# A per-row scalar for GpSimd's head weights, and relus of a score unit that are planned apart

## The reference

```
r = jax.nn.relu(jnp.einsum('bqhe,ble->bqhl', qi, ki_all))
score = jnp.einsum('bqhl,bqh->bql', r, wi)          # wi: one weight per query and head
score = jnp.where(adm, score, -jnp.inf)             # chunk-causal
_, idx = lax.top_k(score, topk)                     # topk = 256
...                                                 # attention over the chosen keys
```

## Time and profile before

| | |
|---|---|
| median of 3 runs | 5120.09 us (5118.19 to 5121.09) |
| profiled execution: span from first to last instruction | 5121.8 us |
| busy in the span: PE, DVE, ACT, POOL | 85%, 68%, 67%, 32% |
| stage one ends, next stage begins | about 2489 us into the span |

### The profile page before, as it was taken

How to read it: one execution, slowest core, us unless ns; L and a number is a source line. 1 busy time by engine, 2 the same in 40 slices (tenths; PEclk the granted TensorE clock), 3 DMA queues, 4 the chain that set the end, 5 groups by cost and what they waited for, 6 DMA issues and landing times. The chain is left out here.

```text
span 5121.8 us, 78325 instructions
## 1 busy us (share of the span) xinstructions
PE 4351.6 (85%) x26505; PEld 2716.9 (53%) x26505; DVE 3484.2 (68%) x6644; ACT 3455.7 (67%) x6887; POOL 1618.2 (32%) x1358
## 2 busy tenths in 40 slices
PE   6767778777677877777689999989999999989999
PEld 3334434443333433434366777767777777754444
DVE  1266778888797988989477777787776778625111
ACT  1578788888697787974378888868788885520100
POOL 1345556666647866677310000000000000000000
PEclk9888889888788888988799999999999999999999
DMA  6211111100011011101421111110110010044422
GB/s 143 61 51 45 38 38 36 35 33 36 22 44 39 33 37 44 42 32 46 152 70 56 51 42 39 40 53 31 34 40 28 28 40 24 12 119 134 118 94 103
DMA packets 201975, 276.98 MB, mean 54 GB/s; under 512 B 50496, under 2 KB 134176, under 8 KB 201056
## 3 DMA queue, kind: packets, MB, share of 16 engines
q1 hardware_dynamic: 198624, 271.81, 16.8%
q10 hardware_dynamic: 2960, 0.17, 0.0%
HBM read 156.73 MB, written 114.16 MB: 53 GB/s over the span
## 5 line engine op out<-in xcount | busy, mean ns | idle before, releaser
L595 PE MATMUL bank<-w,x 128*128 128x512 f32 (+1 forms) x2848 | 1256.8, 597 | 23.6 <-DVE w L940 13.5
L1042 DVE TENSOR_SCALAR_CACHE_REDUCE ties<-score,cand 128x512 int8<-128x512 f32 (+13 forms) x448 | 1110.6, 2479 | 123.2 <-POOL score L916 107.9
L595 PEld LDWEIGHTS bank<-w,x 128*128 128x128 f32 x2848 | 575.9, 206 | 612.7 <-issue 547.4
L806 ACT ACTIVATE act_junk<-score,a_cand,a_sign 128x384 int8<-128x384 f32 (+13 forms) x420 | 879.4, 2094 | 14.0
L1833 DVE CUSTOM_DVE_ANT_0 row<-bank,mask 128x512 f32<-128x512 f32 (+3 forms) x1024 | 622.6, 639 | 179.8 <-PE bank L1572 178.5
L613 PE MATMUL bank<-kiT,qi 128*128 128x512 f32 (+3 forms) x1136 | 395.3, 490 | 408.6 <-ACT relu L736 206.4
L1539 POOL TENSOR_TENSOR near_bias<-table,mask 128x2048 f32<-128x2048 f32 (+1 forms) x32 | 129.5, 4048 | 1763.9 <-DVE part L1833 1748.3
L1767 ACT ACTIVATE pT<-bank 128x512 f32<-128x512 f32 (+2 forms) x704 | 368.7, 524 | 426.2 <-PE bank L1588 424.0
L1669 ACT ACTIVATE row<-row,top 128x1024 f32<-128x1024 f32 (+7 forms) x640 | 632.8, 990 | 4.0 <-DVE top L1846 4.0
L1588 PE MATMUL bank<-ident,row 128*128 128x128 f32 x4224 | 593.7, 281 | 26.4 <-DVE pT L1944 19.5
L1572 PE MATMUL bank<-kT,qb 64*128 64x256 f32 (+1 forms) x4352 | 608.4, 396 | 8.7 <-DVE part L1833 5.4
(11 more groups left out here) (255 smaller groups left out, 4882.6 us busy)
## 6 DMA issues: line engine op xcount, KB each, us to landing
qk_t<-ring SPq DMA_DIRECT2D x66, 256.0 KB, 2.0
gates<-ring SPq DMA_DIRECT2D x66, 256.0 KB, 2.0
gate<-gates SPq DMA_DIRECT2D x33, 512.0 KB, 3.4
out<-x_in SPq DMA_DIRECT2D x33, 512.0 KB, 2.9
x<-in_x_prompt SPq DMA_DIRECT2D x32, 512.0 KB, 3.7
mixed<-mixT SPq DMA_DIRECT2D x64, 256.0 KB, 2.1
mix_in<-mixed SPq DMA_DIRECT2D x32, 512.0 KB, 4.2
x_in<-in_x_prompt SPq DMA_DIRECT2D x32, 512.0 KB, 3.8
```

Source lines behind the costliest of these rows:

```text
L595: ins = pe.matmul(p_bank[n % 2][:, 0:n1 - n0], held[:, c * P:(c + 1) * P], w[:, c, n0:n1], start=(c == 0), stop=(c == KC - 1))
L806: tick(act.activation(junk, row, ACT.Sign, bias=c, scale=back, accum_out=a_sum[:, :]))
L1042: n = tick(dve.tensor_scalar(ties[:, 0:width], row, c.bitcast(F32), 0.0, ALU.is_ge, ALU.add, accum_out=counts[:, i:i + 1]))
```

## The change

The weight is one value per row (a column of 128 values). Before, it is broadcast along the row and used as a second tensor in a `tensor_tensor`; after, it is the scalar operand of a `tensor_scalar`. The additions at L912 stay as they are. In ACT's generator the four relus of a unit get due times that are 1.8 us of planned time apart.

```diff
+RELU_GAP = 1.8
...
-                            for _ in relu_unit(t - 1, slot):
-                                yield us_at(t, slot + 0.6)
+                            for h, _ in enumerate(relu_unit(t - 1, slot)):
+                                yield us_at(t, slot + 0.6) + RELU_GAP * h
...
-                        r, weighs = relu[at % 3][:, 0:n], weight[:, u % 2, h:h + 1].to_broadcast([P, n])
+                        r, weighs = relu[at % 3][:, 0:n], weight[:, u % 2, h:h + 1]
                         pool.wait_ge(s_rl, at + 1)
                         if h == 0:
                             pool.wait_ge(s_wi, u + 1)
-                            pool.tensor_tensor(to, r, weighs, ALU.mult).then_inc(s_pa, 1)
+                            pool.tensor_scalar(to, r, weighs, None, ALU.mult).then_inc(s_pa, 1)
                         else:
-                            k = tick(pool.tensor_tensor(r, r, weighs, ALU.mult))
+                            k = tick(pool.tensor_scalar(r, r, weighs, None, ALU.mult))
                             pool.wait_ge(s_pool, k)
                             pool.wait_ge(s_pa, at)
                             pool.tensor_tensor(to, to, r, ALU.add).then_inc(s_pa, 1)
```

## The result

The changed kernel takes 5223.03 us (median of 4 runs, 5221.86 to 5224.29) against 5120.59 before (median of 4 runs, one more than in the table above): ratio 1.0197, 95% interval 1.0182 to 1.0211. That is 102 us more. The forecast was 5041 us, faster; neither the range nor the sign holds.

The account below looks back on a forecast made before the run. ACT, waiting at relus for POOL, was taken to bound stage one. Gains of 51 us (1305 to 2340), 20 (700 to 1305) and 8 (last step) make 79: 5120 - 79 = 5041 us, range 4965 to 5110.

Parts of the forecast that it names:

- the scalar form is no shorter: Rival on POOL's multiply: a column as scalar may take as long, only the planning acts; 5099 us, chance 0.05.
- the one-column row: Profile row on POOL: a tensor_scalar of one column, 0.19 us elsewhere, took 1.18 us beside a DVE compare.
- the 20-column row: Profile row on POOL: a tensor_scalar of 20 columns, 0.27 us, used in estimating the scalar multiply at 512 columns.
- The path: Stage one, 1305 to 2340: ACT is the path, going over to POOL where ACT stands at a relu, 153 us.
- nearly gone: Sign on ACT: waits behind the first multiply (L907) would nearly vanish; 30 of 35.4 us from 1305 to 2340.
- (c): ACT, 1305 to 2340: ten long waits, 75.8 us, with POOL held beside DVE's scan; planned tests take off 14 us.
- Shifted more than thinned: Planning in ACT's order: a place between tests still has about four relus; counted at nothing.
- (a): ACT, 1305 to 2340: a unit's fourth relu waiting for POOL's first multiply (L907); 30 of 35.4 us go.
- (b): ACT, 1305 to 2340: ordinary waits behind the addition (L912), POOL still at the last unit; 33 of 41.6 us go.
- Slower: evacuations behind the fourth relu: Rival, 150 to 1305: late relus delay evacuations, reaching PE's projection banks and ACT; 5162 us, chance 0.08.
- The waits pass on: Rival, stage one: PE's and DVE's fixed orders take over, only 35 us gained; 5085 us, chance 0.18.

Follow-up runs that it names:

- experiment 1: The two parts separately: the scalar multiply alone, an edit of the changed kernel, 5291.2 us; the planning alone, an edit of the kernel before, 5090.8 us.
- experiment 2: Kernel before with sixteen extra operations on POOL at the start of stage one, 128 and 512 columns, each waited for: 5127.6 us (one run).
- experiment 3: Kernel before with eight other tensor_scalar forms on POOL at the start, 128 and 512 columns, each waited for: column with multiply-add 0.69 us, multiply-max 1.93 us.

## Why the prediction was wrong

**The step that failed** is the price of the scalar multiply. It said 0.72 us, "no more than the addition with two full tensors, 1.27 us" as the upper end. It measured 1.56 us for 512 columns and 0.60 for 128, which is 2.5 ns per column. I had put the 0.88 ns per column of a memset onto a `tensor_scalar` of 20 columns: an operation that only writes lends no slope to one that reads and computes. The upper end rested on the thought that one long input can't cost more than two. Nothing in the trace showed that, and it is false here. With 1.56 the unit is 2.1 us longer, not 1.3 shorter. Even the prediction's own upper end lost 0.9 us per unit, yet no case was made of it: "the scalar form is no shorter" stopped at the same length, so no case held the result. Its sign of being wrong, a multiply of over 1 us, is the one that came. The same place also hid the cure: the one-column row is a two-operation form, the 20-column row a one-operation form, and I used both as if they were one.

The Trainium skill's figure cited there (GPSIMD Engine Reference, Performance versus the Vector engine), 768 ns for 512 elements in a tight loop, is met by neither form: 1.56 us with one operation, 0.69 with two, which is below it. The measurements decide.

**The path was read rightly.** With the multiply at 0.69 us, near the 0.72 of the prediction, and with the planning, the time is 5047 us and the gain 79 us: the forecast 5041 and its 79. Stage one ends at 2406.88, near 2410. Two more of its signs came in that run, from 1305 to 2340: ACT's waits behind the additions are 79.8 us (about 70 forecast), and DVE is busy 915 of 1035 us, 88% (above 87% forecast). The waits behind the first multiply are 20.5 us there, more than "nearly gone". That the sum fits so well is partly luck: the unit by itself gave 56 to 66 us, where the steps say 70 without (c), and the planning gave 13.

**The planning was mis-sized.** I counted it at nothing beside 14 us of (c). It gives 34 us with the old multiply, 64 with the slow one and 13 with the fast one. "Shifted more than thinned" was wrong for what matters: a fourth relu behind a test mostly no longer waits for the first multiply. These waits fell from 133 to 42 in experiment 1. And the gain did not come through (c): with the planning alone, ACT's waits of over 3.5 us behind POOL from 1305 to 2340 sum to 75.4 us, against 75.8 before. With the fast form the sum is 70.5 without the planning and 58.7 with it. (Of the ten waits in that sum one, 6.1 us, stands behind L907 and not L912; the prediction has all ten behind L912. It changes neither (a) nor (b) by more than some 6 us.)

**The rivals.** "Slower: evacuations behind the fourth relu" named the right sign with the wrong mechanism: the planning alone is faster, and a distance of 2.7 with four buffers faster still. ACT does wait more for PE then, 23 us with the planning alone and 21 at 2.7, so late relus may cost something; it never outweighed the gain. "The waits pass on" is partly true: waits for L595 grow by 23 us with the planning alone and by 48 with the fast multiply and planning.

**(c), the long waits beside DVE's scan**: the scalar form does not escape them, as said. In the changed kernel the scalar multiply at 2515.05 took 9.40 us beside a scan of 9.09, and the longest waits of ACT are 11.9 us there and 13.0 with the fast form:

```profile
2513.99 9.09 DVE L972 TENSOR_TENSOR_SCAN score<-ties 128x3840 f32<-128x3840 int8 x1
2515.05 9.40 POOL L908 TENSOR_SCALAR score<-relu,weight 128x512 f32<-128x512 f32 x1
2523.12 4.46 DVE L977 SCALAR_TENSOR_TENSOR ties<-score,pick,ties 128x3840 int8<-128x3840 f32 x1
2524.43 4.58 POOL L910 TENSOR_SCALAR relu<-relu,weight 128x512 f32<-128x512 f32 x1
```

The page SBUF — State Buffer of the Trainium skill (Who interferes with whom) states that a VectorE instruction with two SBUF inputs contends with a GpSimd instruction that reads SBUF. The trace agrees: the scan is given `ties` for both of its inputs, and the multiply with one long input took 9.40 us instead of 1.56.

## What to carry to other kernels

Before an operation is replaced by a "simpler" one on the same engine, find a row of that very form, with its number of operations and its width, or measure it alone: some 18 us of idle GpSimd settled here what no bound from neighbouring rows did. When a slow engine hands small buffers to a fast one, a us more or less on the slow one moved the time by 0.3 to 0.7 us, and the first product of each batch counted somewhat more than the others. A change of two parts may hide a gain: the planning was worth 34 us by itself and stood inside a loss of 102.

## What the runs showed of the hardware

On GpSimd, f32, 512 columns, DVE quiet (experiments 2 and 3): `tensor_scalar` with one operation 1.49 us (immediate, multiply or add) and 1.56 us (column); with multiply-add or multiply-multiply 0.62 us (two immediates) and 0.69 us (column and immediate); with multiply-max 1.93 us. `tensor_tensor` with a broadcast column 1.04 us, with two full tensors 1.26 us; copy 0.61 us. Adding 0.0 as a second operation thus makes a scalar multiply more than twice as fast.

The first `tensor_scalar` of experiment 2 took 3.85 us for 128 columns, where the next took 0.60. DVE was not quiet beside it:

```profile
22.30 3.85 POOL L884 TENSOR_SCALAR relu<-relu 128x128 f32<-128x128 f32 x1
22.51 3.24 DVE L959 TENSOR_SCALAR w<-w,wg 128x512 f32<-128x512 f32 x8
```

In each of three runs POOL's first `tensor_scalar` ends just behind these eight operations of DVE, whatever its own size: at 26.15 against 25.75 here, at 26.77 against 26.52 in experiment 3 (3.68 us long), and at 25.82 against 25.76 in the kernel before, where it has one column and took 2.59 us instead of 0.19. So it looks held off by DVE. A cost of the first use is not shown.
